# Two issuers for the two halves of a weight ring: SyncE for the left half, ScalarE for most of the right

## What is computed

```python
def expert_block(args):
    xi, e = args
    return (jax.nn.silu(xi @ w1[e]) * (xi @ w3[e])) @ w2[e]
```

## Time and profile before

| | us |
|---|---|
| median of three runs | 1141.76 |
| the profiled execution | 1140.18 |
| its span (first to last instruction) | 1138.4 |

### The profile page before, as it was taken

The page is one execution under the profiler, slowest core; times in us unless marked ns, Lnnn a source line. Parts: engine busy times, 40 slices in busy tenths (PEclk is TensorE's granted clock), DMA queues, the critical chain, the costliest instruction groups (busy, mean ns, idle before and its releaser), DMA issues.

```text
span 1138.4 us, 11487 instructions
## 1 busy us (share of the span) xinstructions
PE 849.4 (75%) x5102; PEld 401.6 (35%) x5102; DVE 209.8 (18%) x402; ACT 179.1 (16%) x384; POOL 19.2 (2%) x20
## 2 busy tenths in 40 slices
PE   9999998673958366646799999976565666664776
PEld 7688553221413122212258665322121221221222
DVE  2222231110101001101016544211010101011011
ACT  3323221010100000000036442101010100000002
POOL 0500000000000000000000000000000000000000
PEclk9999998896988779888899999988787888888898
DMA  9972799999999999999995658999999999999996
GB/s 374 422 304 94 282 382 411 430 427 443 441 427 427 436 433 424 440 434 416 423 422 216 273 202 335 419 427 443 431 436 431 433 434 431 437 427 431 434 416 272
DMA packets 23898, 444.48 MB, mean 390 GB/s; under 512 B 3106, under 2 KB 3618, under 8 KB 6563
## 3 DMA queue, kind: packets, MB, share of 16 engines
q1 hardware_dynamic: 23264, 443.15, 92.2%
q10 hardware_dynamic: 578, 0.52, 0.1%
HBM read 442.62 MB, written 1.05 MB: 390 GB/s over the span
## 4 chain that ended last, share of the span: by engine, by line
PE 54%; DMA 40%; ACT 2%; issue 2%; DVE 2%; SPq 0%; DVEq 0%
DMA ring<-in_joined 28%; PE ps L1054 12%; PE ps L1058 10%; DMA ring<-in_last_down 5%; DMA ring<-in_moe_w 5%; PE ps L866 4%; PE ps L1263 4%; PE ps L945 3%; PE ps L1026 3%; PE ps L1040 3%; PE ps L1353 2%; PE ps L952 2%; PE ps L1319 1%; DMA xres<-in_x 1%; PE ps L859 1%
## 5 line engine op out<-in xcount | busy, mean ns | idle before, releaser
L1054 PE MATMUL ps<-ring,work 128*32 128x512 f32 x2032 | 250.3, 648 | 133.2 <-DMA ring<-in_joined 92.1
L1058 PE MATMUL ps<-ring,work 128*32 128x512 f32 (+1 forms) x1024 | 141.4, 712 | 109.1 <-DMA ring<-in_joined 88.3
L1054 PEld LDWEIGHTS ps<-ring,work 128*32 128x32 f32 x2032 | 75.2, 118 | 295.1 <-issue 168.1
L1058 PEld LDWEIGHTS ps<-ring,work 128*32 128x32 f32 x1024 | 39.1, 130 | 200.1 <-issue 192.4
L2084 DVE TENSOR_TENSOR xres<-xres,ps 128x512 f32<-128x512 f32 (+1 forms) x64 | 43.0, 672 | 296.4 <-PE ps L1026 293.8
L1040 PE MATMUL ps<-xs,work 128*128 128x512 f32 x112 | 54.0, 628 | 13.0 <-issue 10.6
L1026 PE MATMUL ps<-work 128*128 128x512 f32 x120 | 55.7, 606 | 0.4 <-ACT work L1640 0.4
L866 PE MATMUL ps<-ring 128*128 128x384 f32 x160 | 53.3, 490 | 0.0
L2075 DVE TENSOR_TENSOR work<-work,ps 128x512 f32<-128x512 f32 x16 | 11.0, 687 | 226.0 <-PE ps L1054 226.0
L1653 ACT COPY work<-ps 128x512 f32<-128x512 f32 x28 | 16.4, 585 | 219.9 <-PE ps L1058 219.9
L1631 ACT COPY work<-ps 128x256 f32<-128x256 f32 x16 | 5.9, 372 | 241.2 <-PE ps L1091 241.2
(11 more groups left out here) (273 smaller groups left out, 688.2 us busy)
## 6 DMA issues: line engine op xcount, KB each, us to landing
ring<-in_moe_w SPq DMA_DIRECT2D x41, 2048.0 KB, 14.6
ring<-in_last_up SPq DMA_DIRECT2D x8, 2048.0 KB, 33.7
ring<-in_moe_w SPq DMA_DIRECT2D x14, 1024.0 KB, 6.8
ring<-in_first_up SPq DMA_DIRECT2D x5, 2048.0 KB, 11.6
ring<-in_out SPq DMA_DIRECT2D x4, 2048.0 KB, 27.4
ring<-in_last_down SPq DMA_DIRECT2D x4, 2048.0 KB, 36.3
ring<-in_queries_keys SPq DMA_DIRECT2D x7, 1024.0 KB, 25.5
ring<-in_first_up SPq DMA_DIRECT2D x4, 1024.0 KB, 7.2
```

The lines of the kernel that those rows point to most:

```text
L1054: return pe.matmul(ps[32 * e:32 * e + 32, 4 + m, :], xsel[:, k, 32 * e:32 * e + 32], w, start=k == 0, stop=k == KC - 1, tile_position=(0, ...
L1058: return pe.matmul(ps[32 * e:32 * e + 32, bank, 0:w.shape[-1]], actT[:, j, 32 * e:32 * e + 32], w, start=j == 0, stop=j == 3, tile_positio ...
```

## The change

A function `by_scalar(l, i)` picks the J that go to the right half, have a J two before them in the same layer, and don't straddle the start of quad 5. SP leaves these out of its loop. ACT issues them instead: `next_right` stands at three places of ACT's quad (once w1, w3 and w2 of the quad have been used), waits for the same `ring_used` count as SP did, and issues the transfer into the same slots with the same semaphore.

```diff
+        def by_scalar(l, i):
+
+            right = (i - FIRST_JOINED[l]) % 2 == (1 if l == 0 else 0)
+            return right and joined_at(l, 0, i - 2) and joined_at(l, 0, i) and not i - 2 < 3 * ROUNDS_AT <= i
+
...
-                            if f % E4 == 0:
+                            if f % E4 == 0 and not by_scalar(l, 3 * g + f // E4):
                                 slot = main[l].slots[n0 + f]
                                 free(l, n0 + f, E4)
...
+            def next_right(rn, c, w):
+
+                l, g = c // NQ, c % NQ
+                i = 3 * g + w + 2
+                if rn is main[l] and by_scalar(l, i):
+                    act_e.wait_ge(ring_used, main[l].used(0, first_fill(l, g) + 4 * w + 4))
+                    act_e.dma_start(ring[:, RIGHT * SLOT:(RIGHT + E4) * SLOT],
+                                    joined[l, i - FIRST_JOINED[1]]).then_inc(ring_in[RIGHT], 16)
+
...
                 act_e.wait_ge(rn.ring_used, rn.used(pair, n0 + 4))
+                if rn is not extra:
+                    next_right(rn, c, 0)
                 nc.scalar.activation(sg, ps[:, 4, :], ACT.Sigmoid).then_inc(rn.sig.sig_done, 1)
                 act_e.wait_ge(rn.sig.selT_mm, c + 1)
                 nc.scalar.copy(selwT.rearrange("p a t -> p (a t)"), ps[:, 2, 0:T]).then_inc(rn.sig.selwT_ready, 1)
+                if rn is not extra:
+                    next_right(rn, c, 1)
...
                     nc.scalar.copy(yb[:, half * 512:half * 512 + 512], ps[:, 6 + half, :]).then_inc(rn.sig.yb_ready, 1)
+                if rn is not extra:
+                    next_right(rn, c, 2)
```

## The result

| | before | after |
|---|---|---|
| median, us | 1141.2 (four runs) | 1165.62 (four runs) |
| all runs, us | 1140.43 to 1142.06 | 1164.21 to 1169.92 |
| the profiled execution, us | 1140.18 | 1165.91 |
| its span, us | 1138.4 | 1164.1 |

The ratio is 1.0224 (95% interval 1.0208 to 1.024). The forecast of 1151.5 and its range up to 1158 were too low. Rival B, the full walk of 21.7 us at 1163, came nearest; its chance was 0.11, and the range left it out.

What follows compares the result with a forecast made beforehand. The prediction took the DMA engines as the bound, with no idle time to fill. Second-layer idle places summed to 10.3 us, other terms 0: 1140.18 + 10.3 = 1150.5, plus 1.6 for the median, 1152, rounded to 1151.5; range 1140 to 1158.

Steps and rivals of the forecast that it cites:

- Rival B: DMA engines, second layer: rings take turns without delay, costing the full 21.7 us, time 1163; chance 0.11.
- What bounds the kernel: Both expert stretches: DMA engines never run dry, share 1.00 at 433 GB/s, so no idle time for a second issuer.
- ScalarE's own cost, taken as 0: ScalarE's eleven added issues of 0.33 to 0.34 us: 0 to 0.6 us for each, taken as 0.
- Turns, packet by packet: DMA engines alternate between SyncE's and ScalarE's rings after each packet, each ring entering 2 to 3 us late.
- Rival A: DMA engines: J(i+2) begins only when J(i+1) is through, order as before, 1141.8, not slower; chance 0.29.
- The first layer, 0: First layer, sharing from J11 on: no idle DMA time, cost 0, bound 3 us.
- The places in the second layer: Second layer: seven places where DMA engines idle: 1.9, 2.3, 4.2, 0.9, 4.2, 4.0 and 4.2 us.
- walk without late entry: Second layer stepped through once, rings taking turns without delay: idle places sum to 21.7 us.
- It takes 2.4 off each of the five shared places: Second layer: one packet's delayed entry cuts 1.9, 2.3, 4.2, 4.2, 4.2 to 0, 0, 1.8, 1.8, 1.8; sum 10.3 us.
- The late entry: A transfer joining a busy DMA engine waits 2 to 3 us, one packet of a J (2.4 us).
- 1.8 us for a start into idle engines: DMA restart after running dry: overhead of one packet row's start and landing, taken as 1.8 us, between 1.0 and 2.8.
- the prediction's limit for its entry: Second ring's transfer joining busy DMA engines: forecast counted as wrong if entry takes more than 4 us.

## Why the prediction was wrong

**What bounds the kernel: right.** The DMA engines did, and nothing was there to win.

**ScalarE's own cost, taken as 0: right.** The issues take 0.33 to 0.36 us, and with ScalarE as sole issuer inside one ring the landings stay 19.36 apart.

**Turns, packet by packet: right.** In after, from 806 to 810 (packets, MB, share):

```profile
q1 hardware_dynamic: 14, 0.92, 53.0%
q10 hardware_dynamic: 13, 0.85, 49.2%
```

Rival A, with J8 behind J7, is out. The Trainium skill ("DMA: Bandwidth & Descriptors", "Queues, rings and completion order") has each engine drain a packet of some 9 to 17 descriptors before it turns; here the turn came after one row of 64 KB, which the profile counts as one packet (how many descriptors it is, no trace shows). Its sentence in "Issuing engines are not separate DMA queues", that a second issuer only saves the sequencer's time, agrees with this kernel in that nothing was won, but by it the time would have stayed, and the measured 24 us decide.

**The first layer, 0: right,** though five of ScalarE's eleven transfers share there. From 300 to 340:

```profile
q1 hardware_dynamic: 167, 8.85, 51.2%
q10 hardware_dynamic: 126, 8.26, 47.8%
```

**The places in the second layer: right.** Each is where the walk has it. A J's last completion packet, after against before, gives the loss so far:

| J, and its last completion (after; before) | late by, us | step | walk without late entry | forecast |
|---|---|---|---|---|
| J10 (877.3; 874.5) | 2.8 | 2.8 | 1.9 | 0 |
| J12 (919.3; 913.2) | 6.1 | 3.3 | 2.3 | 0 |
| J15 (985.5; 971.8) | 13.7 | 7.6 | 5.1 | 2.7 |
| J16 (1007.9; 991.1) | 16.8 | 3.1 | 4.2 | 1.8 |
| J18 (1051.2; 1030.8) | 20.4 | 3.6 | 4.0 | 4.0 |
| the span's end (1164.1; 1138.4) | 25.7 | 5.3 | 4.2 | 1.8 |

**The step that failed** is "It takes 2.4 off each of the five shared places". The walk without it gives 21.7 and follows the measured steps within 2.5 us each; with it, the forecast of 10.3 is short at every place but one. The late entry itself is real: the newcomer's first row starts 3.5 to 4.1 us after its issue where the other ring is busy (five of ScalarE's six, two of SyncE's), and 0.9 to 1.0 where the engines are idle. Queues of after from 804.9 to 808.1, after ScalarE's issue at 804.48, and then to 810:

```profile
q1 hardware_dynamic: 19, 1.25, 89.9%
...
q10 hardware_dynamic: 13, 0.85, 103.6%
q1 hardware_dynamic: 1, 0.07, 8.0%
```

What I left out is that the lead is handed back at the end. The last data of J9 are through at about 863; its completions are small packets, and they too wait for a turn, behind a 64 KB row of J10. No packet starts in 863.8 to 864.9, then in 865.2 to 866.2:

```profile
q10 hardware_dynamic: 15, 0.98, 226.7%
q1 hardware_dynamic: 15, 0.00, 0.8%
```

(0.98 MB are fifteen rows; 0.00 MB are fifteen completions.) The last of J9's is through at 867.3, and PE starts on J9 at 868.03. J11, which shares with J12, shows it more plainly: its sixteen last rows start in 906 to 907.4, sixteen rows of J12 in 908.4 to 909.8, and only then, in 910.8 to 912.2, its completions:

```profile
q1 hardware_dynamic: 16, 1.05, 172.8%
...
q10 hardware_dynamic: 16, 1.05, 172.8%
...
q10 hardware_dynamic: 16, 1.05, 172.7%
q1 hardware_dynamic: 16, 0.00, 0.6%
```

At these two pairs one turn of 2.4 us at the end of the first transfer undoes the 2.4 that I had credited at its start.

**A second term was too small**: 1.8 us for a start into idle engines, "between 1.0 and 2.8". The two runs that isolate it give 3.9 and 4.3. I had worked it out from one transfer's landing, which shows the start and the end, but not that sixteen engines out of step all wait for the slowest. As a rough estimate, 2.1 more at each of the walk's seven places, put in before the late entry is taken off, makes the forecast 24.4; the walk without late entry is 21.7; the runs say 24.4. Either correction alone comes near (that the first hits the number is luck), and both in full, 36, are too much. How they divide is open: after a shared pair, the slowest engine's lag and the completion's turn are partly the same microseconds, and no run took the completion's turn away alone.

**The range** ended at 1158 because rival B had 0.11. Its case against was one row, gate_ups, which shows the entry of a transfer and nothing of its completion: I took a lead at one end of the transfer for a lead at both. (The sum gives 1152.1; the 1151.5 that it was rounded to is a slip of 0.6 us, which decides nothing.)

## What to carry to other kernels

Where two transfers in flight depend on places that are handed back one by one, put them in one ring: in order, the first lands as early as it can, its place comes back early, and the queue stays full. In two rings both land late and close together; here that cost nothing in the first layer, where the engines didn't run dry, and some 4 us for each of six in the second, where they did. Before crediting any overlap, walk the pairs with the consumer's times, and price each start into idle DMA engines by a run of its own.

## What the runs showed that I had not expected

- A start into idle DMA engines costs 3.9 to 4.3 us of a stream that otherwise never stops, though only 1.4 us pass without data. The first 64 KB row takes some 3.1 us instead of 2.42 on each of the sixteen engines.
- A completion of a few bytes takes its own turn behind the other ring's 64 KB row: at J9 and J11 2.4 us from a transfer's last data to its completions.
- A newcomer's first row starts 3.5 to 4.1 us after its issue if another ring is busy, 0.9 to 1.0 if none is (the prediction's limit for its entry was 4).
- A J in four transfers with 16 KB rows moves at 427 GB/s, in one with 64 KB rows at 433, with the DMA share at 1.00 in both: 8.0 us over this kernel.
- Nothing here beats the kernel before: no run in this study was faster, and its DMA share leaves no idle time in the joined stretches to win.
